# Another order of the matmuls in the up projections: one output tile after the other instead of both side by side

## The reference

```
def conv_ffn(h, w_up, w_conv, b_conv, w_down):        # D_FF = 2816, twice
    u = h @ w_up                                       # 256x1024 @ 1024x5632
    u = depthwise_conv3(u, w_conv) + b_conv
    val, gate = jnp.split(u, 2, axis=-1)
    return (jax.nn.silu(gate) * val) @ w_down

def shortconv_mixer(h, w_in, conv_w, w_out):           # WIDTH = 1536
    u = h @ w_in                                       # 256x1024 @ 1024x6144
    bg, cg, xv, gate = four parts of u
    y = bg * causal_depthwise_conv(cg * xv, conv_w)
    return (y * jax.nn.silu(gate)) @ w_out
```

## Time and profile before

| what | value |
|---|---|
| runs | 887.05, 888.56 and 889.69 us; median 888.56 us |
| the profiled execution | 887.05 us |
| its span, first to last instruction | 885.3 us |
| TensorE busy | 856.8 us, 97% of the span |
| DVE, ACT, POOL busy | 670.2, 547.9, 26.2 us |
| mean granted TensorE clock | 0.994 of 2.4 GHz |

### The profile page before, as it was taken

The page is one execution under the profiler, slowest core; times in us unless marked ns, Lnnn a source line. Parts: engine busy times, 40 slices in busy tenths (PEclk is TensorE's granted clock), DMA queues, the critical chain, the costliest instruction groups (busy, mean ns, idle before and its releaser), DMA issues.

```text
span 885.3 us, 13300 instructions
## 1 busy us (share of the span) xinstructions
PE 856.8 (97%) x4833; PEld 743.7 (84%) x4833; DVE 670.2 (76%) x923; ACT 547.9 (62%) x745; POOL 26.2 (3%) x60
## 2 busy tenths in 40 slices
PE   8999889999999999998999999999999999999996
PEld 8977778888888878877888888879999788888886
DVE  6898748887777778867888777768877677776763
ACT  5754556756556566565675655668988765554442
POOL 2000100000000011010000000000000000000000
PEclk9999999999999999998999999999999999999999
DMA  8553624564554525225556455526354046545521
GB/s 324 189 212 119 234 95 160 198 214 188 190 205 174 191 91 194 88 103 214 213 195 215 184 190 192 188 96 238 118 221 185 0 144 237 202 174 217 185 77 47
DMA packets 22440, 152.74 MB, mean 173 GB/s; under 512 B 2528, under 2 KB 2656, under 8 KB 5120
## 3 DMA queue, kind: packets, MB, share of 16 engines
q1 hardware_dynamic: 22032, 149.71, 46.0%
q0 software_dynamic: 368, 2.49, 0.7%
HBM read 151.14 MB, written 1.05 MB: 172 GB/s over the span
## 4 chain that ended last, share of the span: by engine, by line
PE 85%; DVE 5%; ACT 3%; issue 1%; DMA 1%; POOL 0%; SPq 0%; ACTq 0%; DVEq 0%; POOLq 0%
PE acc L1689 26%; PE ring L1637 25%; PE ring L1641 13%; PE ring L1676 9%; PE acc L1902 2%; PE ring L1884 1%; DVE w_lo L920 1%; PE ring L2061 1%; PE acc L1585 1%; PE ring L1654 1%; PE ring L1942 1%; DMA raw<-in_stream_dram 1%; ACT w_hi L472 1%; ACT xn L487 1%; DVE x L985 0%
## 5 line engine op out<-in xcount | busy, mean ns | idle before, releaser
L920 DVE TENSOR_TENSOR w_lo<-raw,w_hi 128x2048 fp32r<-128x2048 f32 (+1 forms) x146 | 320.1, 2196 | 9.7 <-ACT w_hi L472 9.6
L1637 PE MATMUL ring<-hh,w_hi 128*128 128x512 f32 x992 | 311.5, 395 | 0.6 <-DVE usum L1006 0.4
L472 ACT ACTIVATE w_hi<-raw 128x2048 fp32r<-128x2048 f32 (+1 forms) x146 | 266.8, 1841 | 51.0 <-DMA raw<-in_stream_dram 47.3
L1641 PEld LDWEIGHTS ring<-hh,w_lo 128*128 128x128 f32 x992 | 186.3, 188 | 43.8
L1641 PE MATMUL ring<-hh,w_lo 128*128 128x256 f32 x992 | 194.9, 278 | 0.0
L1637 PEld LDWEIGHTS ring<-hh,w_hi 128*128 128x128 f32 x992 | 153.1, 189 | 3.4 <-issue 0.7
L1689 PE MATMUL acc<-w_hi,a_hi 128*128 128x512 f32 x264 | 103.4, 392 | 0.5 <-DVE a_lo L1221 0.5
L1689 PE MATMUL acc<-w_lo,a_hi 128*128 128x512 f32 x264 | 103.0, 390 | 0.0
L1689 PE MATMUL acc<-w_hi,a_lo 128*128 128x512 f32 x264 | 102.7, 389 | 0.0
L1006 DVE TENSOR_TENSOR usum<-ring,usum 128x512 f32<-128x512 f32 x65 | 44.8, 690 | 74.2 <-ACT usum L477 74.2
L1676 PE MATMUL ring<-hh,w_hi 128*128 128x256 f32 x512 | 93.5, 285 | 0.0
(11 more groups left out here) (243 smaller groups left out, 923.5 us busy)
## 6 DMA issues: line engine op xcount, KB each, us to landing
raw<-in_stream_dram SPq DMA_DIRECT2D x134, 1024.0 KB, 4.8
raw<-in_stream_dram SPq DMA_DIRECT2D x12, 512.0 KB, 3.6
gatew<-in_gatew_dram POOLq DMA_DIRECT2D x1, 1536.0 KB, 7.0
x<-in_x_dram SPq DMA_DIRECT2D x2, 512.0 KB, 3.6
out_dram<-xn SPq DMA_DIRECT2D x2, 512.0 KB, 2.6
row<-in_row_dram POOLq DMA_DIRECT2D x1, 640.0 KB, 9.2
gup_raw<-in_gup_dram SPq DMA_DIRECT2D x3, 128.0 KB, 13.7
par<-in_par_dram SPq DMA_DIRECT2D x1, 274.0 KB, 4.6
```

The lines of the kernel that those rows point to most:

```text
L472: nc.scalar.activation(w_hi[:, u % RING, 0:n], raw[:, u % RAW, 0:n], ACT.Copy).then_inc(hi_split, 1)
L920: nc.vector.tensor_tensor(w_lo[:, u % RING, 0:n], raw[:, u % RAW, 0:n], w_hi[:, u % RING, 0:n].bitcast(f32), ALU.subtract).then_inc(lo_spl ...
L1637: nc.tensor.matmul(ring[:, 2 * k + f, :], w_hi[:, u % RING, lo:lo + P], hh[:, kc, :, :], start=kc == 0, stop=False, skip_group_check=True)
L1641: last = nc.tensor.matmul(ring[:, 2 * k + f, 0:S], w_lo[:, u % RING, lo:lo + P], h_hi[:, kc, :], start=False, stop=kc == KC - 1, skip_grou ...
```

## The change

In `merged`, the loop over the output tile f becomes the outer one and the loop over kc the inner one, and the second loop over f is gone. The same 32 matmuls with the same operands and flags run in another order: before, two long ones (tiles 0 and 1) and then two short ones (0 and 1) for each kc; now one long and one short in turn, eight pairs for tile 0 and then eight for tile 1. The waits ahead of the unit and the `used` on its last matmul stay. Nothing else in the kernel changes.

```
-                for kc in range(KC):
-                    for f in range(2):
+                for f in range(2):
+                    for kc in range(KC):
                         lo = kc * 256 + f * P
                         nc.tensor.matmul(ring[:, 2 * k + f, :], w_hi[:, u % RING, lo:lo + P], hh[:, kc, :, :],
                                          start=kc == 0, stop=False, skip_group_check=True)
-                    for f in range(2):
-                        lo = kc * 256 + f * P
                         last = nc.tensor.matmul(ring[:, 2 * k + f, 0:S], w_lo[:, u % RING, lo:lo + P], h_hi[:, kc, :],
                                                 start=False, stop=kc == KC - 1, skip_group_check=True)
                 last.then_inc(used, 1)
```

## The result

The changed kernel is slower. Its runs took 895.21 to 896.67 us, median 895.38, against a median of 889.12 for the kernel before (887.05 to 890.09, four runs each). The ratio is 1.0077, with a 95% interval of 1.0055 to 1.0098: 6.3 us. I had forecast 888.2 us, with 891.5 as the upper end.

A forecast was written before the change was run, and what follows sets the result against it. The spacing of TensorE's matmul starts was taken to bound the kernel. The terms summed to 0 us, with 1.9 us either way; a lean of minus 0.4 us from the median of 888.56 gave 888.2 us, range 884.5 to 891.5.

The forecast's parts named there:

- What bounds the kernel: Whole kernel: TensorE, busy 856.8 of 885.3 us, sets the time by the distance between its matmul starts.
- What the change can't do: Around the merged units: no read, split or load starts earlier and waits stay as they are; 0 us.
- the banks: Merged units: 16 matmuls in a row on one bank cost nothing; short directly behind long on the same columns remained a possible loss.
- What a unit costs: Merged unit: 5.550 us from pure runs, plus 0.01 to 0.03 us for the mix, 0.6 to 1.9 us in the span.
- the charge is laid on per short matmul: Merged units: each short matmul costs some 6 ns over half a long one; their number stays, so change 0 us.
- Weight loads: Merged units: each step keeps two loads behind long matmuls, with time to spare, and two behind short ones, without; cost 0.
- Rival 2: Merged units: length changes, or short ones awaiting long ones' columns, cost about 15 ns each; plus 7.4 us, 896.0; chance 0.10.
- Rival 1: Merged units: a short matmul between long ones costs half a long one; unit 5.451 us, gain 7.4, time 881.2; chance 0.14.
- The chances: Whole kernel: faster by over 0.3% 0.14, same 0.76, slower 0.10.
- The inner range: Whole kernel, case of no change: 885.6 to 890.8 us, from 1.9 us of the mix and 1.5 us of run scatter.

The follow-up runs named there:

- the swapped order: Against the kernel before, the two short matmuls of each step swapped, tile 1 first; 889.42 us, ratio 0.9998.

## Why the prediction was wrong

**What bounds the kernel: right.** TensorE's spacing in the merged units sets the time; the loss of 6.3 us appears there and just behind. No wait came or went: 1.1 us idle ahead of line 1637.

**What the change can't do: right.** Nothing is released earlier; ACT's waits for the short matmuls' line went from 66.7 us to 74.2, as fits a slower TensorE. And the banks cost nothing. For the case that no row covered, a short one directly behind a long one on the same columns, the swapped order shows 0.

**What a unit costs, the term that failed.** The pure runs were right, 5.550 us for a unit; all long ones first gives 5.555. The failing step is the one after it: "this is all that depends on how long and short ones stand among each other". I took the 1 to 4 ns that the one known mixture had over the sum, and let it at most double. It measured (5.645 - 5.550) / 8 = 12 ns a step in turn against (5.57 - 5.55) / 8 = 2.5 in pairs: nearly five times, not twice. With it falls the reading behind it, "the charge is laid on per short matmul": the same 16 short ones now stand in a unit that is 0.08 us longer. The unit had been forecast at 5.55 to 5.58 us and the two mean durations at 673 ns together; they came out at 5.65 us and 679. A bound for a new order cannot be had from the surplus of another order. The only mixture in the trace was the pattern in pairs, and by the later runs that was a mild one by luck.

**Weight loads: "Cost 0", wrong.** I counted tight and roomy loads, found two and two in both orders, and concluded that nothing changes. That count assumes that a tight load costs the same wherever it stands. In turn, halving the tight load (and the outputs that go with it) changes two units by 0.38 us; in pairs the same edit changes them by 0.05, the other way. The sum had no term for it.

**Rival 2, given one chance in ten, had the right time.** It gave 896.0 us, measured were 895.4, and it named the length changes as the place. Its price was worked out as a linear cost per change, 15 ns each; there it was right only in the total, by luck. It asked for units of 5.69 us and got 5.64 to 5.65, with the rest in the down units; and one change in place of eight brought nothing. My argument against it, that a wide unit without changes pays 6 ns for each short one too, was sound for the order in pairs and said nothing of the order in turn. Its other half, a short one that waits for the columns of the long one ahead, was wrong: the swapped order shows no such cost.

**Rival 1** forecast a unit of 5.451 us for the order in turn, and this is what it takes once all loads and outputs of the merged units are halved, 5.45. Its idea was not absurd, but with full loads the sign is the opposite.

**The chances.** Nothing in the trace showed a lone short matmul between long ones. The rows allowed minus 7.4 to plus 7.4 us, and I put three quarters on the middle because the known order was additive. With the ends at equal distance and no row of the new pattern, both should have weighed more, and the range should have reached the price of rival 2. The inner range was loose too: its half-width of 2.6 us is not the sum of the 1.9 and 1.5 us that it names.

## What to carry to other kernels

Where TensorE is busy without gaps, the order of matmuls of different length is a cost of its own, here 3 ns on each of 2,000 matmuls and 0.7% of the kernel, even when no wait comes or goes and the banks play no part. If an order is to be changed, keep the pattern of lengths (long long short short, tile by tile, cost nothing) or measure the new pattern; pure runs don't bound it. And the cost of a pattern shows in the trace as the length of one unit to 0.01 us, long before it can be told from a few runs of the whole kernel.

## What the runs showed of the hardware that I had not expected

- Long and short matmuls in turn, 512 and 256 columns with full weight loads: 353 ns a pair, against 348 in pairs and 347 from pure runs. With 384 for 256 the order in turn is the better one, 13.00 against 13.18 us.
- With the load behind the short matmul cut to 64 columns, and the outputs with it, the order in turn streams at the rate of long matmuls, 341 ns a pair; with all loads at 96 columns it doesn't, 353.
- The slowdown outlasts the unit by about ten matmuls, 0.05 us of a down unit.
- Matmuls directly behind one another on one bank and the same columns cost nothing extra, whatever their lengths (11.14 us with and without).
